# Gate block 3 leaves its banks one scan step sooner, and two pieces of gate block 1 go ahead of the turned rows

## What is computed

```python
def mamba2_mixer(h, norm_w, in_w, conv_w, conv_b, dt_bias, a_log, d_skip, gnorm_w, out_w):
    u = rms_norm_2(h, norm_w)
    zxbcdt = u @ in_w
    z, xbc, dt = jnp.split(zxbcdt, [D_INNER, D_INNER + CONV_CH], axis=-1)
    ...
    xbc = jax.nn.silu(xbc)
    xs, bm, cm = jnp.split(xbc, [D_INNER, D_INNER + SSM_GROUPS * D_STATE], axis=-1)
    ...
    y = ssd_chunked(xs, dt, a, bm, cm)
    y = y + d_skip.astype(jnp.float32)[:, None] * xs.astype(jnp.float32)
    y = y.reshape(b, s, D_INNER) * jax.nn.silu(z.astype(jnp.float32))
    yg = y.reshape(b, s, SSM_GROUPS, D_INNER // SSM_GROUPS)
    yg = yg * lax.rsqrt(jnp.mean(yg * yg, axis=-1, keepdims=True) + EPS)
    y = yg.reshape(b, s, D_INNER) * gnorm_w.astype(jnp.float32)
    return y.astype(h.dtype) @ out_w
```

## Time and profile before

| what | value |
|---|---|
| time, median of 3 runs | 954.23 us (953.45 to 956.28) |
| profiled execution: time, span | 955.79 us, 954.0 us |
| TensorE matmul (PE) busy | 917.3 us, 96% |
| TensorE weight load (PEld) busy | 804.8 us, 84% |
| VectorE (DVE) busy | 678.6 us, 71% |
| ScalarE (ACT) busy | 523.3 us, 55% |
| GpSimd (POOL) busy | 74.4 us, 8% |
| mean granted TensorE clock | 0.995 of 2.4 GHz |
| time in the chain that ended last, on PE | 62% of the span |

### The profile page before, as it was taken

One profiled execution on the slowest core, in us unless ns is written; L12 is line 12 of the kernel. 1 busy time (PEld: TensorE's weight loads), 2 busy tenths in 40 slices (PEclk: granted clock), 3 DMA queues, 4 the chain that ended last, 5 costly groups with the idle time before them and its releaser, 6 DMA issues.

```text
span 954.0 us, 14498 instructions
## 1 busy us (share of the span) xinstructions
PE 917.3 (96%) x5721; PEld 804.8 (84%) x5721; DVE 678.6 (71%) x969; ACT 523.3 (55%) x784; POOL 74.4 (8%) x75
## 2 busy tenths in 40 slices
PE   6999999999999989999999899989989998999998
PEld 6998998988888769999988699978878786878777
DVE  6688737874878678888854677893567687876665
ACT  7862332234445366666543565865666668477543
POOL 5002422420000000000000000003000000000000
PEclk9999999999999999999999999999999999999999
DMA  9543132122455455565555455542312453632231
GB/s 308 167 162 101 45 117 86 47 71 95 168 196 170 159 181 177 182 197 194 179 180 190 160 177 161 185 146 90 123 53 91 155 208 105 216 132 89 89 106 71
DMA packets 80979, 136.63 MB, mean 143 GB/s; under 512 B 3957, under 2 KB 46545, under 8 KB 80912
## 3 DMA queue, kind: packets, MB, share of 16 engines
q1 hardware_dynamic: 78800, 131.17, 41.4%
q0 software_dynamic: 2112, 4.53, 1.5%
HBM read 134.64 MB, written 1.05 MB: 142 GB/s over the span
## 4 chain that ended last, share of the span: by engine, by line
PE 62%; ACT 7%; DVE 5%; issue 4%; DMA 2%; DVEq 0%; ACTq 0%
PE bank L437 17%; PE bank L439 17%; PE bank L438 17%; PE bank L426 3%; ACT upper L1275 2%; DVE lower L1842 1%; PE bank L1078 1%; PE bank L883 1%; DVE arena L2383 1%; PE bank L1062 1%; PE bank L892 1%; ACT arena L1374 1%; DMA loaded<-in_ssm_in_w 1%; ACT arena L1758 1%; PE bank L684 1%
## 5 line engine op out<-in xcount | busy, mean ns | idle before, releaser
L1842 DVE TENSOR_TENSOR lower<-loaded,upper 128x2048 fp32r<-128x2048 f32 x122 | 278.4, 2284 | 135.2 <-ACT upper L1275 133.0
L1275 ACT ACTIVATE upper<-loaded 128x2048 fp32r<-128x2048 f32 x122 | 232.0, 1904 | 117.8 <-PE bank L439 104.7
L437 PE MATMUL bank<-xT_upper,upper 128*128 128x256 f32 (+1 forms) x664 | 188.5, 284 | 1.3 <-DVE xT_lower L1907 1.3
L438 PE MATMUL bank<-xT_lower,upper 128*128 128x256 f32 (+1 forms) x664 | 186.9, 281 | 0.0
L439 PE MATMUL bank<-xT_upper,lower 128*128 128x256 f32 (+1 forms) x664 | 186.8, 281 | 0.0
L437 PE MATMUL bank<-upper,xT_upper 128*128 128x512 f32 (+1 forms) x360 | 146.2, 406 | 6.2 <-DVE lower L1842 3.4
L439 PE MATMUL bank<-upper,xT_lower 128*128 128x512 f32 (+1 forms) x360 | 139.5, 387 | 0.0
L438 PE MATMUL bank<-lower,xT_upper 128*128 128x512 f32 (+1 forms) x360 | 139.0, 386 | 0.0
L437 PE MATMUL bank<-upper,split_arena 128*128 128x512 f32 x296 | 121.5, 411 | 6.5 <-DVE arena L2437 3.6
L437 PEld LDWEIGHTS bank<-xT_upper,upper 128*128 128x128 f32 (+1 forms) x664 | 125.5, 189 | 2.4 <-issue 2.2
L438 PEld LDWEIGHTS bank<-xT_lower,upper 128*128 128x128 f32 (+1 forms) x664 | 127.2, 192 | 0.1
(11 more groups left out here) (342 smaller groups left out, 1199.4 us busy)
## 6 DMA issues: line engine op xcount, KB each, us to landing
loaded<-in_w_in SPq DMA_DIRECT2D x26, 1024.0 KB, 5.1
loaded<-in_ffn_w_up SPq DMA_DIRECT2D x22, 1024.0 KB, 5.1
loaded<-in_ssm_in_w SPq DMA_DIRECT2D x20, 1024.0 KB, 5.3
loaded<-in_ffn_w_down SPq DMA_DIRECT2D x11, 1024.0 KB, 4.8
loaded<-in_ssm_out_w SPq DMA_DIRECT2D x8, 1024.0 KB, 4.9
loaded<-in_ple_gate_w SPq DMA_DIRECT2D x8, 1024.0 KB, 5.1
loaded<-in_attn_in_w SPq DMA_DIRECT2D x8, 1024.0 KB, 5.2
loaded<-in_w_branch_ret SPq DMA_DIRECT2D x4, 1024.0 KB, 4.9
```

Source lines behind the costliest of these rows:

```text
L437: mm(out, a[0], b[0], start=start, stop=False)
L438: mm(out, a[0], b[1], start=False, stop=False)
L1275: A(part(upper, PARTS, n), part(loaded, LOADS, n), ACT.Copy).then_inc(uppers, 1)
L1842: TT(part(lower, LOADS, n), part(loaded, LOADS, n), part(upper, PARTS, n).bitcast(F32), sub) \
```

## The change

- `z_piece` takes only its own bank, in the piece with `half == 0`, in place of both banks in the first piece of a block.
- On TensorE the second piece of block 1, (1, 0, 1), moves from behind the turns of `bR` to ahead of them and of the wait for `xbc_ready`; the third, (1, 1, 0), moves from behind `cb` to ahead of it.
- ScalarE's two tanh of block 3 move from step 7, behind the exponentials, to the end of step 6.
- VectorE's two gate instructions of block 3 move from the end of step 7 to the end of step 6.

```diff
             def z_piece(j, half, i, ready=False, between=None):
-                if half == i == 0:
-                    z_banks[j] = [take(pe, key, 2 * (j % 2) + m) for m, key in enumerate(z_keys(j))]
+                if half == 0:
+                    z_banks[j, i] = take(pe, z_keys(j)[i], 2 * (j % 2) + i)
...
-                    last = mm3(z_banks[j][i][:, :], both(xT, every, 4 * half + k, slice(i * P, i * P + P)),
+                    last = mm3(z_banks[j, i][:, :], both(xT, every, 4 * half + k, slice(i * P, i * P + P)),
                                both(w, every, k, every), half + k == 0, half == 1 and k == 3)
...
             z_piece(1, 0, 0)
+            z_piece(1, 0, 1)
             pe.wait_ge(sem("xbc_ready"), 24)
             turns(("bR",), 5, [xbc[:, 16 + g, 0:P] for g in range(4)])
-            z_piece(1, 0, 1)
+            z_piece(1, 1, 0)
             for n in range(2):
                 ps = take(pe, ("cb", n), 6 + n)
...
                 fill(last, ("cb", n))
-            z_piece(1, 1, 0)
             emptied(pe, ("bR",))
             pe.wait_ge(sem("xd_ready"), 2)
             states(0)
...
-                if z in (4, 7):
-                    z_tanh(2 if z == 4 else 3)
+                if z == 4:
+                    z_tanh(2)
                 if z in SPLIT:
                     split_to(SPLIT[z], -1)
...
                 if z % 4 == 2 and g:
                     group_upper(g - 1, 0)
                     group_upper(g - 1, 1)
+                if z == 6:
+                    z_tanh(3)
...
-                if z in (4, 7):
+                if z in (4, 6):
                     gate_rows(2 if z == 4 else 3)
```

## The result

The changed kernel took 949.31 us (median of 13 runs, 946.57 to 952.36), the kernel before 954.42 on the same chip (13 runs, 952.51 to 957.54). The ratio is 0.9944, with a 95% interval of 0.993 to 0.9958, which is about 5.3 us less, where 4.9 was forecast. The profiled execution took 951.35 us, with a span of 949.5.

The account below looks back on a forecast made before the run. TensorE, busy 96% of the span, was taken as the bound, so only gaps and slow stretches on the last-ending chain count. 2.8 + 2.1 = 4.9 us off the 954.2 us median gave 949.3 us, range 947.8 to 951.9.

Parts of the forecast that it names:

- Sum: Whole kernel: 2.8 us from the early gate pieces plus 2.1 from the output tiles, 4.9 us in all.
- Front, 2.8: Gate pieces of block 1: single banks and two pieces ahead of the turns let the states start 2.8 us sooner.
- Back, 2.1: In out_tile(0), earlier gates remove a 3.59 us wait; after a new wait, group 1's second turns gain 2.1 us.
- The new wait: Before group 1's first turns, TensorE would wait 2.2 us for scaled rows, and some 0.8 before the second turns.
- Step 6: Earlier place with the same instructions: turns 0.54 and second turns 4.55 us behind the rows, used to price group 1.
- the row at 546.00: Matmul after a 2.21 us idle without lower clock, taken as nearest sign that the clock holds in the new wait.
- The rival, at 17 in 100: The clock falls once in the wait before group 1's turns, costing 0.5 to 1.3 us: 950.4 us; 17 in 100.
- The prediction's last sentence: Signs of error: TensorE idle before the states, turns over 1 us off, or low clock at the new wait.
- The rule of the Trainium skill: Short idles between matmul groups suffice to make the clock go back and forth; by it the gain is 3.6 us.
- Only one half: Only the early pieces gain (951.4 us) or only the output tiles gain (952.1 us); 13 in 100.
- Slower by a clock that goes back and forth: New waits make the clock alternate through the output tiles, 703 to 745; half of it low gives 957.7; 3 in 100.
- The change doing nothing: The change doesn't do what it says, the old wait going on only if the tanh were late; under 1 in 100.

Follow-up runs that it names:

- e1_front: Changed kernel with tanh and gates of block 3 back in step 7, so only banks and piece order differ from before; 952.49 us, ratio 0.9968.
- e4_order_only: Kernel before with two gate pieces of block 1 ahead of the turns, the first still taking both banks; 952.84 us, ratio 0.997.
- e3_banks_only: Kernel before with each gate piece taking only its own bank, piece order and block 3's tanh and gates unchanged; 954.14 us, ratio 0.9987.
- e7_tanh_only: Changed kernel with VectorE's gates of block 3 back in step 7, ScalarE's tanh staying in step 6; 952.33 us, ratio 0.9973.
- e0_same: Changed kernel measured again without any edit, to look at the clock; 949.47 us, ratio 0.9945.
- e2_back: Kernel before with only block 3's tanh and gates moved to step 6, banks and pieces as before; 952.13 us, ratio 0.9972.
- e8_gates_only: Changed kernel with ScalarE's tanh of block 3 back in step 7, VectorE's gates staying in step 6; 947.34 us, ratio 0.9926.
- e0b_same: Changed kernel measured a third time without any edit; 951.08 us, ratio 0.9962.
- e6_joins_first: Changed kernel with VectorE's joins and gated(1, 1) ahead of the lower part of the weight unit in step 8; 947.61 us, ratio 0.9925.
- e6b_joins_first: Second measurement of the changed kernel with step 8's joins ahead of the lower part of the weight unit; 947.32 us, ratio 0.9927.
- e10_all_joins_first: Changed kernel with VectorE's joins and gated ahead of the lower weight part in steps 4, 8 and 12; 946.2 us, ratio 0.9913.
- e9_filled: Changed kernel with eight extra matmuls on TensorE, no part of the result, in the wait before group 1's turns; 950.08 us, ratio 0.9942.

## Why the prediction was right

- **Sum.** 4.9 forecast, 5.3 measured (4.0 to 6.7 by the interval). The front half of it holds as it was put; the back half holds in its mechanism, but its size rested on a course of the clock that mostly didn't come. That the time itself came out at 949.31 where 949.3 was forecast is partly chance: the median of the runs shown, 954.23, and that of the runs beside the changed kernel, 954.42, could have lain further apart.
- **Front, 2.8.** Measured 2.95 and 2.75. Its steps hold: bank 2 is free in time, the second piece meets a free bank 3, no idle ahead of the turns, the states start at once, and `xdd` isn't late. So does the sentence that splitting the take alone gives nothing (states 13.58 with the banks alone), and that the lead is kept.
- **Back, 2.1.** The wait is gone and the gates are ready. The new wait is 2.03, forecast 2.2. The second one was put at 0.8 and is 0.58 where the clock held. First turns 2.98 earlier, forecast 708.58 - 705.7 = 2.9. Second turns 2.2 earlier where the clock held, forecast 2.1. Step 6, as the row to go by, was within 0.2 each time. But 711.82 - 709.7 sets a course with a low stretch against one without, so 2.1 holds some 0.9 of clock. The second turns, by the wait ahead of them and by what the clock did, show the move by itself:

  | | no low stretch | low for 3.4 us | low for 6.8 us |
  |---|---|---|---|
  | old wait, 3.5 to 3.6 | 17.17 (`e1_front`) | 18.07 (before), 18.23 (`e4_order_only`) | 19.43 (`e3_banks_only`), 19.19 (`e7_tanh_only`) |
  | new wait, 2.0 to 2.1 | 15.88 (`e0_same`) | 16.39 (`e2_back`), 16.69 (changed), 16.75 (`e8_gates_only`) | 17.88 (`e0b_same`) |
  | no wait over 0.3 | 13.69, 13.66, 13.69 (`e6_joins_first`, `e6b_joins_first`, `e10_all_joins_first`) | none | none |

  From the first row to the second, the move is worth 1.3 us without a low stretch, 1.3 to 1.8 with one of 3.4, and 1.3 to 1.6 with one of 6.8.
- **What the sum didn't split.** VectorE's and ScalarE's moves were costed as a pair. All of the back but 0.1 comes from VectorE's.
- **The clock: the step that failed.** "I take no fall: one idle is nearest to the row at 546.00." The clock fell in the new wait in 4 of 5 profiles that have it unfilled: the changed kernel, `e2_back` and `e8_gates_only` with 3.4 us, `e0b_same` with 6.8; not in `e0_same`. The low stretch began in the wait (`e2_back`, `e0b_same`) or up to 1.5 us behind its end and cost the second turns 0.5 (16.39), 0.8 (16.69), 0.9 (16.75) and 2.0 (17.88), against 15.88. The rival, at 17 in 100, had said 0.5 to 1.3: in the profiles it was the rule, and once it cost more. The prediction's last sentence names a low stretch at the new wait as a sign of being wrong, and on this step it was. The error is in the reasoning too: one row with a fall and one without show that such an idle may go either way, and were read as if the nearer row decided. The row at 546.00 isn't even sure in itself: the same wait of 2.2 us was followed by the lower clock in 8 of the 14 profiles (last section). The rule of the Trainium skill ("TensorE: Matmul & The Clock Gate", section "A second HAM failure mode: psum-queue depth-cycling") was nearer to it, in that a short idle was enough; its back and forth through the output tiles isn't in any profile: at most one stretch, of 3.4 or 6.8 us, stands there.
- **Why the median was met all the same.** The clock fell at the old wait too, in 4 of the 5 profiles that have it, so low stretches are in both medians. The profiles show the place in one execution each, but every execution's mean granted clock is known: on average 0.9924 in 70 executions of the kernel before, 0.9936 in 32 of the changed kernel (standard errors 0.0002 and 0.0005). That is some 2.3 us less at the lower level for each execution, and at the forecast's 0.4 for each us an estimate of 0.9. With 2.75 to 2.95 for the front and 1.3 to 1.8 for the back it makes 5.0 to 5.7, around the 5.3 measured. By this estimate, less time at the lower level somewhere in the execution gave what the sum had booked at the new wait. That is luck in part, and it isn't shown that the edit caused it.
- **Rivals.** Only one half: refuted by both halves alone. Slower by a clock that goes back and forth: not in any profile. The change doing nothing: no.

## What to carry to other kernels

When an in-order engine waits for several buffers at once, look at when each comes free, and then at what could fill the time won: either edit alone may be worth nothing, as the banks alone were here. When a wait is taken away, follow the chain of the next wait in the trace of before and price it with the same instructions elsewhere in the kernel; here that gave the new wait to 0.2 us. The row ahead of it in the queue (a 2.28 us weight part that nobody needed yet) was the next edit, worth 2 us more. When a slow stretch of the clock stands in the profile of before, take it out of the sum, or leave it in on both sides. Judge an edit of a few microseconds by distances between two instructions around it, and by medians, not by the spans of two profiles.

## What was not expected of the hardware

**The clock after an idle isn't decided by its length alone.** The old wait of 3.51 to 3.61 was followed by the 1.2 GHz level in 4 of 5 profiles (before, `e3_banks_only`, `e4_order_only`, `e7_tanh_only`; not `e1_front`), the new wait of 2.03 to 2.13 in 4 of 5. The wait on which the forecast leaned, ahead of 546.00 in the trace of before, is 2.20 to 2.22 in all 14 profiles, in code that no variant touches, and a low stretch began in it or up to 0.9 us behind it in 8 of them. In the changed kernel it stands at 541.46, and its row lasts 0.69 where that of before lasts 0.51:

```profile
541.46 0.69 PE L437 MATMUL bank<-upper,xT_upper 128*128 128x512 f32 x1 [2.20 <-DVE lower L1844]
```

The pair of 1.35 and 1.26 near 800 was followed by one in 8 of 14 as well. Where the waits at the place of the change are at most 0.6 (`e6_joins_first`, `e6b_joins_first`, `e10_all_joins_first`, `e9_filled`), no low stretch stood there in any of the four profiles, and their 24 executions have a mean granted clock of 0.9950, above the 0.9936 of the changed kernel. That speaks for closing or filling such a wait, though no single pair of runs shows it. The low stretches at this place were 3.4 us or 6.8 us long. What decides between two executions is open.

**The same matmuls have two paces.** The products of 128x256 between about 360 and 474 us, 969 of them with no wait among them, start every 117.8 ns in some profiles and every 113.3 ns in others, at a granted clock of 1.00 in both. From the first start to the last it is 114.0 us (before, `e0_same`, `e0b_same`, `e6_joins_first`, `e9_filled`) or 109.7 us (the changed kernel, `e1_front` to `e4_order_only`, `e6b_joins_first`, `e7_tanh_only`, `e8_gates_only`, `e10_all_joins_first`). The same window of two profiles of one and the same code, `e6_joins_first` and then `e6b_joins_first`:

```profile
400.00:430.00 30.00, 30.00 (x257) 30.00 (x256) 25.66 (x38) 19.25 (x30) 0.00 (x0) 1.00 0.60 198
```
```profile
400.00:430.00 30.00, 30.00 (x267) 30.00 (x267) 26.94 (x42) 17.98 (x28) 0.00 (x0) 1.00 0.59 192
```

257 matmuls in one, 267 in the other, PE always busy. It isn't the code and it isn't the granted clock, DMA does nearly as much in both, and two of the three chips of the experiments showed both paces. The gain of 4.3 us isn't kept in full: from there to the last channel matmul those at 113.3 ns need 155.6 to 158.1 us and those at 117.8 ns 155.3 to 155.7. All of the former but `e10_all_joins_first` have a stretch of low clock that begins between 541 and 546. That one kept the gain (155.6). It also had no low stretch near 800. Both are in its profiled execution, 941.58, which lies 4.6 below its own median. What sets the pace is open; it wasn't tried.
